# Two-layer transformer block on one core: four of the 22 weight steps of each FFN output tile pair by Strassen's seven products

## What is computed

```python
D_MODEL, SEQ, D_FF = 2048, 256, 5632
def conv_ffn(h, w_in, conv_w, conv_b, w_out):
    u = h @ w_in                              # [256, 2*5632]
    ...                                       # three taps along the tokens
    g, val = c[..., :D_FF], c[..., D_FF:]
    return (gelu(g) * val) @ w_out            # [256, 5632] @ [5632, 2048]
f = conv_ffn(rms_norm(x, ffn_norm_pre[l]), ffn_w_in[l], ...)
x = x + rms_norm(f, ffn_norm_post[l])
```

## Time and profile before

| what | value |
|---|---|
| median of 3 executions | 2181.61 us (2181.32 to 2182.11) |
| profiled execution, span from first to last instruction | 2179.6 us |
| the profiled execution's own time | not listed beside the three; its span lies 2.0 us under their median |
| FFN output product, layer 0 and layer 1 | from 854.4 us and from about 1932 us of the span, 88 steps each |
| PE busy | 2168.8 us |
| DVE, ACT, POOL busy | 1453.7, 1225.8, 6.8 us |

### The profile page before, as it was taken

The page is one execution under the profiler, slowest core; times in us unless marked ns, Lnnn a source line. Parts: engine busy times, 40 slices in busy tenths (PEclk is TensorE's granted clock), DMA queues, the critical chain, the costliest instruction groups (busy, mean ns, idle before and its releaser), DMA issues.

```text
span 2179.6 us, 32913 instructions
## 1 busy us (share of the span) xinstructions
PE 2168.8 (100%) x11685; PEld 1879.3 (86%) x11685; DVE 1453.7 (67%) x2048; ACT 1225.8 (56%) x1708; POOL 6.8 (0%) x20
## 2 busy tenths in 40 slices
PE   9999999999999999999999999999999999999998
PEld 8989988888888888888888889888888888888887
DVE  5757756776777767444489877567677777764444
ACT  5745745565566565443365567466556656554443
POOL 0000000000000000000000000000000000000000
PEclk9999999999999999999999999999999999999999
DMA  8565265556565656656656544655656665565554
GB/s 288 178 186 184 78 214 172 184 174 204 180 190 186 194 184 202 209 188 199 193 165 203 197 150 130 201 162 183 202 174 199 183 196 182 183 221 195 194 194 151
DMA packets 201505, 406.11 MB, mean 186 GB/s; under 512 B 12925, under 2 KB 13303, under 8 KB 200655
## 3 DMA queue, kind: packets, MB, share of 16 engines
q1 hardware_dynamic: 200687, 400.29, 58.1%
q0 software_dynamic: 736, 4.72, 0.6%
HBM read 402.86 MB, written 2.10 MB: 186 GB/s over the span
## 4 chain that ended last, share of the span: by engine, by line
PE 98%; DVE 1%; ACT 0%; DMA 0%; issue 0%; SPq 0%; DVEq 0%
PE ps L589 42%; PE ps L635 29%; PE ps L643 15%; PE ps L673 4%; PE ps L683 3%; PE ps L1295 1%; PE ps L764 1%; PE ps L1195 0%; PE ps L894 0%; PE ps L736 0%; PE ps L829 0%; PE ps L900 0%; PE ps L923 0%; PE ps L837 0%; DVE x L2575 0%; PE ps L862 0%
## 5 line engine op out<-in xcount | busy, mean ns | idle before, releaser
L2146 DVE TENSOR_TENSOR w_lo<-w_raw,w_hi 128x1024 fp32r<-128x1024 f32 x608 | 736.8, 1223 | 475.3 <-ACT w_hi L1491 470.9
L1491 ACT ACTIVATE w_hi<-w_raw 128x1024 fp32r<-128x1024 f32 (+1 forms) x624 | 645.1, 1046 | 454.5 <-PE ps L589 326.5
L635 PE MATMUL ps<-xT,w_hi 128*128 128x512 f32 x2752 | 657.7, 391 | 0.0
L635 PEld LDWEIGHTS ps<-xT,w_hi 128*128 128x128 f32 x2752 | 505.4, 188 | 98.3 <-issue 0.4
L643 PEld LDWEIGHTS ps<-xT,w_lo 128*128 128x128 f32 x2752 | 353.1, 191 | 13.8 <-DVE w_lo L2146 0.4
L643 PE MATMUL ps<-xT,w_lo 128*128 128x256 f32 x2752 | 358.2, 283 | 0.0
L589 PE MATMUL ps<-w_hi,hT_hi 128*128 128x512 f32 x704 | 273.9, 389 | 0.0
L589 PE MATMUL ps<-w_hi,hT_lo 128*128 128x512 f32 x704 | 273.9, 389 | 0.0
L589 PE MATMUL ps<-w_lo,hT_hi 128*128 128x512 f32 x704 | 273.9, 389 | 0.0
L589 PE MATMUL ps<-w_hi,xT 128*128 128x512 f32 x640 | 203.3, 392 | 0.0
L589 PEld LDWEIGHTS ps<-w_hi,hT_hi 128*128 128x128 f32 x704 | 132.2, 188 | 27.5
(11 more groups left out here) (307 smaller groups left out, 2148.9 us busy)
## 6 DMA issues: line engine op xcount, KB each, us to landing
w_raw<-in_ffn_w_in SPq DMA_DIRECT2D x352, 512.0 KB, 4.0
w_raw<-in_ffn_w_out SPq DMA_DIRECT2D x176, 512.0 KB, 4.6
w_raw<-in_shared_w_kv SPq DMA_DIRECT2D x48, 512.0 KB, 4.3
w_raw<-in_a_w_o SPq DMA_DIRECT2D x32, 512.0 KB, 4.7
w_raw<-in_b_w_in SPq DMA_DIRECT2D x32, 512.0 KB, 4.6
w_raw<-in_b_w_o SPq DMA_DIRECT2D x32, 512.0 KB, 4.5
w_raw<-in_a_w_mem_kv SPq DMA_DIRECT2D x16, 512.0 KB, 6.0
w_raw<-in_b_w_mem_kv SPq DMA_DIRECT2D x16, 512.0 KB, 4.5
```

Of the source, the lines that this page charges most:

```text
L635: mm = nc.tensor.matmul(ps[:, base + m4, :].rearrange("p (a n) -> p a n", a=2), w_hi[:, slot, cols], xT[:, :, 2 * k + c, :], start=k == c ...
L1491: nc.scalar.activation(w_hi[:, s % R, 0:width], w_raw[:, s % R, 0:width], ACT.Copy)\
L2146: nc.vector.tensor_tensor(w_lo[:, s % R, :], w_raw[:, s % R, :], w_hi[:, s % R, :].bitcast(F32), ALU.subtract)\
```

## The change

In each layer the four output tiles form two pairs. For steps 0 to 3 (`PAIRS = 4`) of a pair, the two steps of its two tiles, which share their rows of `w_out`, become a unit: a product of 2x2 blocks (two chunks, two token halves, two column tiles) that is made of seven block products in the place of eight. A unit is four entries: *left* (two block products on the step of the left tile as it lies), *corner* (one, on a 512-wide quarter of the right tile's step), *odd* (two, on two sums of quarters) and *even* (two, on two more sums). GpSimd forms the odd sums (`odd_sums_of`), DVE the even ones from them. The sums lie where `w_lo` of the same slot will be written. The other 18 steps of each tile stay plain. `out_order` writes the order: nine plain steps of the pair's left tile, four units with two plain steps after each of the first three, the last three plain steps, then 18 plain steps of the right tile: 104 entries for 88 loads (`OUT_RAWS`) in a layer. A fifth slot (`w5_hi`, `w5_lo`) joins the ring from the first unit of a pair for 40 entries (`out_slots`).

Matching sums of activations (`sx_hi`, `sx_lo`) are made in the first two iterations of the FFN input loop: four subtractions and additions of 128x256, one 128x1024 subtraction on DVE, one 128x1024 copy on ACT, an iteration. They lie where `x` lies, so GpSimd sends `x` (2 MB) to HBM before that loop (`x_leaves`) and fetches it after the last unit (`x_returns`); ACT waits for the first before the loop, DVE for the second before the last tile is added to `x`. The seven products of a unit add to banks 4, 2, 0, 1, 6, 5 and 3; after a pair's last unit ACT copies two of them and DVE does five 128x512 operations (`fold`), for which PE waits before the pair's right tile, and one of 128x1024 later. In the core of the diff, `...` marks what is left out:

```diff
+PAIRS = 4
...
+def out_order():
+    entries, raws = [], []
+    def plain(tile, k):
+        entries.append(("plain", tile, k, len(raws)))
+        raws.append((tile, k, "entry", len(entries) - 1))
+    def unit(half, p):
+        r = len(raws)
+        entries.extend((kind, 2 * half, p, r) for kind in ("left", "corner", "odd", "even"))
+        for tile in (2 * half, 2 * half + 1):
+            raws.append((tile, p, "unit", half * PAIRS + p))
+    ends, unit_ends, unit_starts = [], [], []
+    for half in range(2):
+        ks = list(range(PAIRS, FSTEPS))
+        for k in ks[:CUT]:
+            plain(2 * half, k)
+        rest = ks[CUT:]
+        unit_starts.append(len(entries))
+        for p in range(PAIRS):
+            unit(half, p)
+            if p == PAIRS - 1:
+                unit_ends.append(len(entries))
+            n = 2 if p < PAIRS - 1 else len(rest)
+            for k in rest[:n]:
+                plain(2 * half, k)
+            rest = rest[n:]
+        ends.append(len(entries))
+        for k in ks:
+            plain(2 * half + 1, k)
+        ends.append(len(entries))
+    return entries, raws, ends, unit_starts, unit_ends
+OUT_ENTRIES, OUT_RAWS, OUT_ENDS, UNIT_STARTS, UNIT_ENDS = out_order()
+OSTEPS = len(OUT_ENTRIES)
+EXTRA = OSTEPS - len(OUT_RAWS)
+WIDE = 40
...
+def out_slots():
+    slots, users, last = [], [], {k: k - R for k in range(R)}
+    last[R] = -1
+    for e in range(OSTEPS):
+        slot = e % R
+        for e0 in UNIT_STARTS:
+            if e0 <= e < e0 + WIDE:
+                slot = ((e0 + (e - e0) % (R + 1)) % R) if (e - e0) % (R + 1) < R else R
+        slots.append(slot)
+        users.append(last[slot])
+        last[slot] = e
+    assert all(slots[e] == e % R for e in list(range(CUT)) + list(range(OSTEPS - R + 1, OSTEPS)))
...
+            def out_weights(s_out, name, layer):
+                for r, (j, k, _, _) in enumerate(OUT_RAWS):
+                    if r < R:
+                        sp.wait_ge(lo_ready, s_out + r - R + 1)
+                    elif OUT_RAWS[r - R][2] == "entry":
+                        sp.wait_ge(lo_ready, s_out + OUT_RAWS[r - R][3] + 1)
+                    else:
+                        sp.wait_ge(unit_sums, layer * UNITS + OUT_RAWS[r - R][3] + 1)
+                    sp.dma_start(w_raw[:, r % R, :].rearrange("p (c n) -> p c n", c=2),
+                                 view[name][:, 2 * k:2 * k + 2, 512 * j:512 * (j + 1)])\
+                        .then_inc(w_landed[r % R], 16)
...
+            def x_leaves(pieces):
+                pool.wait_ge(x_piece, pieces)
+                pool.dma_start(x_kept, x[:, :, :].rearrange("p t n -> p (t n)")).then_inc(x_spilled, 16)
+            def x_returns(s_out):
+                pool.wait_ge(step_used, s_out + UNIT_ENDS[1])
+                pool.dma_start(x[:, :, :].rearrange("p t n -> p (t n)"), x_kept).then_inc(x_back, 16)
+            def odd_sums_of(s0):
+                for e, (kind, _, _, r) in enumerate(OUT_ENTRIES):
+                    if kind == "odd":
+                        for no in (raw_no(s0) + r, raw_no(s0) + r + 1):
+                            pool.wait_ge(w_landed[no % R], 16 * (no // R + 1))
+                        pool.wait_ge(step_used, s0 + OUT_USERS[e] + 1)
+                        quarters = unit_quarters(r)
+                        nc.gpsimd.tensor_tensor(
+                            out_slot(e)[2].rearrange("p (a n) -> p a n", a=2), quarters[:, 0:4:3, :],
+                            quarters[:, 2].unsqueeze(1).to_broadcast([P, 2, 512]), ALU.add)\
+                            .then_inc(odd_sums, 1)
...
+                def unit(e, kind, p):
+                    wh, wl, _ = out_slot(e)
+                    a, b = slice(0, 512), slice(512, 1024)
+                    def h(c, t, cols, bank):
+                        return terms(bank, hT_hi[:, 2 * p + c, tok_t[t]],
+                                     hT_lo[:, 2 * p + c, tok_t[t]], wh[:, cols], wl[:, cols])
+                    def s(form, cols, bank):
+                        o = 256 * form + P * (p % 2)
+                        return terms(bank, sx_hi[:, p // 2, o:o + P], sx_lo[:, p // 2, o:o + P],
+                                     wh[:, cols], wl[:, cols])
+                    if kind == "left":
+                        h(0, 0, a, 4)
+                        return h(1, 0, b, 2)
+                    if kind == "corner":
+                        return s(3, a, 0)
+                    if kind == "odd":
+                        s(0, a, 1)
+                        return s(1, b, 6)
+                    s(2, a, 5)
+                    return h(1, 1, b, 3)
+                for half in range(2):
+                    release(t0 + 2 * half)
+                    begun.clear()
+                    first = OUT_ENDS[2 * half - 1] if half else 0
+                    for e in range(first, OUT_ENDS[2 * half]):
+                        kind, j, k, _ = OUT_ENTRIES[e]
+                        if e == UNIT_STARTS[half]:
+                            release(t0 + 2 * half + 1)
+                            if half == 0:
+                                pe.wait_ge(pair_act, t0)
+                                pe.wait_ge(pair_dve, t0)
+                                pe.wait_ge(s_lo, (PAIRS // 2) * (layer + 1))
+                            else:
+                                pe.wait_ge(folded, 4 * layer + 2)
+                        pe.wait_ge(lo_ready, s0 + e + 1)
+                        if half == 0 and k == FSTEPS - 2:
+                            pe.wait_ge(h_lo, h_done)
+                        mm = plain(e, k, 2, range(TT)) if kind == "plain" else unit(e, kind, k)
+                        mm.then_inc(step_used, 1)
+                    pe.wait_ge(folded, 4 * layer + 2 * half + 1)
...
+                hi, _, sums_now = out_slot(e)
+                if kind in ("plain", "left", "corner"):
+                    r += kind == "corner"
+                    no = raw_no(s0) + r
+                    act.wait_ge(w_landed[no % R], 16 * (no // R + 1))
+                elif kind == "odd":
+                    act.wait_ge(odd_sums, units + UNITS // 2 * (e >= OUT_ENDS[1]) + p + 1)
+                else:
+                    act.wait_ge(unit_sums, units + UNITS // 2 * (e >= OUT_ENDS[1]) + p + 1)
...
+            def fold_copies(s0, half):
+                splits_to(s0 + UNIT_ENDS[half] + 4)
+                act.wait_ge(step_used, s0 + UNIT_ENDS[half])
+                nc.scalar.activation(fold_now[:, 0], ps[:, 1, :], ACT.Copy)
+                nc.scalar.activation(fold_kept[:, 0], ps[:, 4, :], ACT.Copy).then_inc(fold_copied, 1)
...
+                dve.wait_ge(hi_ready, s + 1)
+                if kind == "corner":
...
+                    quarters, odd, even = unit_quarters(r), out_slot(e + 1)[2], out_slot(e + 2)[2]
+                    dve.wait_ge(step_used, s0 + OUT_USERS[e + 2] + 1)
+                    dve.wait_ge(odd_sums, unit_no)
+                    nc.vector.tensor_tensor(even[:, 0:512], odd[:, 0:512], quarters[:, 3], ALU.add)\
+                        .then_inc(even_sum, 1)
+                    dve.wait_ge(even_sum, unit_no)
+                    nc.vector.tensor_tensor(even[:, 512:1024], even[:, 0:512], quarters[:, 1],
+                                            ALU.add).then_inc(unit_sums, 1)
             def split(s, per=0, i=None):
...
+            def fold(s0, folds, half):
+                splits_to(s0 + UNIT_ENDS[half] + 4)
+                dve.wait_ge(fold_copied, folds // 2 + 1)
+                p1, u3, q5, u2 = (fold_kept[:, 0], fold_kept[:, 1], fold_now[:, 0], fold_now[:, 1])
+                nc.vector.tensor_tensor(ps[:, 0, :], ps[:, 0, :], q5, ALU.add)
+                link(nc.vector.tensor_tensor(u2, ps[:, 5, :], p1, ALU.add))
+                nc.vector.tensor_tensor(ps[:, 0, :], ps[:, 0, :], u2, ALU.subtract)
+                link(nc.vector.tensor_tensor(u3, ps[:, 6, :], u2, ALU.add))
+                nc.vector.tensor_tensor(ps[:, 1, :], ps[:, 1, :], u3, ALU.subtract)\
+                    .then_inc(folded, 1)
+                splits_to(s0 + OUT_ENDS[2 * half] + AHEAD)
+                dve.wait_ge(step_used, s0 + OUT_ENDS[2 * half])
+                nc.vector.tensor_tensor(ps[:, 2:4, :], ps[:, 2:4, :], fold_kept, ALU.add)\
+                    .then_inc(folded, 1)
```

More of the change, by code:

```diff
@@ L61 @@
 FJ = F // 512
+def out_order():
[44 more added lines that the diff above has]
+    assert all(slots[e] == e % R for e in list(range(CUT)) + list(range(OSTEPS - R + 1, OSTEPS)))
+    assert EXTRA % R == 0 and OSTEPS % R == 0
+    return slots, users
+OUT_SLOTS, OUT_USERS = out_slots()
+UNITS = 2 * PAIRS
 MEMA, MEMA_T = 0, 0
@@ L484, in _ @@
                     tile(s_in + DSTEPS, f"ffn_w_in{layer}", DSTEPS, i * 512 + F, 2 * DSTEPS, i)
-                with sp.Fori(0, 2) as i:
-                    for j in range(2):
-                        tile(s_out + j * FSTEPS, f"ffn_w_out{layer}", FSTEPS,
-                             i * 1024 + 512 * j, 2 * FSTEPS, i)
```

(38 more changed lines are left out.)

261 lines of the change are left out of this document (196 added, 65 removed).

## The result

| | before | the change |
|---|---|---|
| median of 6 executions each | 2181.87 us | 2189.8 us (2188.78 to 2191.4) |
| ratio, with its 95% interval | | 1.0037 [1.0027, 1.0048] |
| profiled execution: its time, its span | span 2179.6 | 2189.9, span 2188.0 |

What follows compares the result with a forecast made beforehand. TensorE, busy 2168.8 of 2179.6 us, was taken as the bound. Terms -10.9 + 15.6 + 2.4 + 0.8 gave +7.9, a span of 2187.5 and a median of 2189.5 us; range 2172.5 to 2199.

Steps and rivals of the forecast that it cites:

- The gain: Output products: 16 units save three matmuls each, 48 at 0.2267 us, so 10.9 us off PE.
- The shared door: GpSimd and DVE with two SBUF inputs share one access to SBUF, so one waits for the other; chance 0.56.
- GpSimd's sum: GpSimd's 128x1024 odd sum in a unit, priced at 2.3 us, bounded by 1.2 and 4.3.
- The circle's excess: Later units: loads, GpSimd's sum and even sums take 11.5 us against PE's 10.2; 1.3 us, 12 times, 15.6.
- the one-way wait: Later units: only GpSimd waits, DVE's corner low half runs beside its sum; excess 0.75 us, 9.0 in all.
- First unit: First unit of each pair: even sums wait for their slot, odd low half comes late; 0.6 us, 4 times, 2.4.
- Fold: Before a pair's right tile PE waits for the fold, about 0.2 us, 4 times, 0.8.
- The return of `x`: Fetching `x` after the last unit costs nothing: more than 50 us of matmuls before its reader, weight loads have slack.
- no shared door: Rival at the units: GpSimd adds beside DVE, circle of 10.15 us closes unseen; -7.7, so 2173.9 us; chance 0.33.
- GpSimd slow: Rival at the units: GpSimd's sum takes 4.3 us; +39, 2220 us; chance 0.08.
- the store late: Rival before the second layer's input loop: storing `x` takes 22 us, ACT starts late; 2192 us; chance 0.03.
- The fourth: Rival at the units: loads land in 3.7 us, door shared, excess 0.5; -2.5, 2179 us; no separate chance given.

Runs made afterwards that it cites:

- The version in which none of the new waits is left: Changed kernel with odd sums on DVE, another slot order, `x` back in eight pieces and activation sums formed earlier: 2171.34 us, ratio 0.9951 against the kernel before.
- the memset version: Changed kernel with GpSimd's odd sums left out, two 128x1024 memsets writing a constant in their place: 2175.75 us, ratio 0.9972 against the kernel before.

## Why the prediction was right, and where it was wrong

- **The gain**, -10.9: right. The version in which none of the new waits is left has 10.5.
- **The shared door**: right, and in both directions, which the rows before could not show. The corner's low half stretches from 0.69 to 2.89 beside the sum. The Trainium skill's page "SBUF — State Buffer", section "Who interferes with whom", says that a VectorE instruction with two SBUF inputs contends with a GpSimd instruction that reads SBUF and not with one that only writes it, and that the shared pair of ports is an exclusive lock. The traces agree with the lock (2.20 us of wait for DVE, 0.84 for GpSimd), and nothing in them speaks against the condition of *reading*, since the memset, which only writes, blocked nothing.
- **GpSimd's sum**, 2.3: measured 2.39. Eight times the shorter selection held. The Trainium skill's "GPSIMD Engine Reference", section 3.1, has 4497 ns for 2048 elements; the estimate of 2.25 us from its half is 0.14 too low.
- **The circle's excess**, 1.3 x 12 = 15.6: too large. Measured 8.3 us of waits (0.69 a unit), 0.11 of each given back; the mean turn of 10.78 is 0.58 over PE's 10.2, where 11.5 was forecast. The term that was mis-sized is the landing of a unit's *first* load, put at 4.8 after the even sums (the median of 4.6, and 0.2 for the handover). In the twelve turns it came 4.1 to 4.6 after them. In the turn shown, the left low half therefore ends at 6.45 and not 7.15 (898.74 - 892.29), and GpSimd's sum, which waits for its end, at 8.7 and not 9.5. In the mean of the twelve the early load is worth 0.5 us of the 0.7; the remaining 0.2 lie in the steps behind the left low half. The second load was forecast too late as well, 6.3 for 5.3 to 5.8, but that cost nothing: in the forecast and in the run it has landed before the left low half is done. The 9.0 of the one-way wait lies nearer to the measured 8.3 than the 15.6 does, but by accident, since the corner's low half does wait.
- **First unit**, 0.6 x 4 = 2.4: too small, 4.1. The chain was right: even sums start at 880.10 and the odd low half reaches PE at 882.71, 2.61 us for 2.65. PE's side was wrong. "After 9 matmuls, 2.04" was counted from the release of the slot, but a release comes when the last matmul has ended, 0.39 us after its start, and by then the next entry's weight loads have begun (879.68). PE asks for the odd entry at 881.72, 1.6 us after the release. Moving the slot took all four waits away, so the slot is the cause.
- **Fold**, 0.8: no wait; 0. In the first pair it ends 11.1 us after the last even sums (924.68 - 913.54) and not 12.25, the loads having come sooner than forecast.
- **`x` to HBM**, 0: right. **The return of `x`**, 0: wrong, the one mechanism that was missed, 5.5 us of waits and 1.6 of clock. This is the step that failed by its mechanism and not by its size. The prediction looked at the return's own reader ("more than 50 us of matmuls before its reader") and granted the weights 3 us of delay out of "steady state". The delay was 5 us, and the ring was not in a steady state, having just come through four units.
- **Activation sums in the input loop**, 0 with a bound of 4: 1.2.

So the overestimate of 7.3 at the units and 0.8 at the fold was paid back by 1.7, 7.1 and 1.2 that were too low elsewhere; the 2.4 that the waits give back and the 1.0 that is open lie between the terms and the total. That the total fits to 0.3 us was luck. The circle and its port were no luck: each of the twelve later units showed them. But they do not carry the loss. The version with the return in pieces has all the causes that were forecast and not the one that was missed, and it takes 2182.72 us, the time of the kernel before within the noise. The forecast causes use up the gain; that the change is *slower*, by 8 us, hangs on the return of `x`, for which the forecast had nothing. So the direction was right in part by luck too. Of the rivals, *no shared door* fell by the corner's 2.89, *GpSimd slow* by the 2.39, *the store late* by the absence of any wait. The fourth, *loads sooner with the door shared*, came true in part: with loads at 3.7 it has an excess of 0.5 a unit, and 0.58 was measured.

## What to carry to other kernels

Before work is handed to an idle engine, ask whether it can run beside its neighbours: here VectorE did in 1.22 us, without a wait, what GpSimd did in 2.39 while blocking VectorE for 2.20. A transfer whose reader has plenty of time can still make others late: split it, and do not send it when the ring that shares the DMA engines is at its emptiest. And cost a small wait at a recurring place against the ones behind it, since a stream that is late once hands the lateness on; four small edits turned 8 us of loss into 10.5 of gain.

## What the runs showed of the hardware

- VectorE with two SBUF inputs and GpSimd with an addition from SBUF exclude each other for whole instructions, and the port changes hands between them: 0.69 becomes 2.89, 2.39 becomes 3.23. A GpSimd memset of 128x1024 (0.95 us) beside the same VectorE instructions stretched neither.
- A 2 MB transfer from GpSimd's queue beside 512 KB weight loads doubles their landing, 4.6 to 9.9 us at 396 GB/s and a DMA share of 1.0 (1040 to 1044 us); in eight pieces it leaves them at 5.3. Whether TensorE waits for them depends on what has been split ahead: with landings of 10.7 and 10.8 us it did not wait in the memset version.
- The granted clock fell after some waits of PE and not after others of the same length. In the changed kernel it fell to 0.61 after 2.3 us idle in layer 0 and stayed at 1.00 after 2.5 us in layer 1. With the sums formed twice it was 0.50 after an idle time of 3.1 us at 2140.81 and stayed at 1.00 after 2.8 us at 1052.27 and after 3.4 us that ended at 2117.68. The length of the one wait does not decide it by itself; what else does was not tested and stays open.
